# State-space tables of a two-block transformer kernel: read-out powers formed in the first feed forward, lags by shifted identities, drive tables in four buffers

## The reference, cut to what matters

```python
def modulation(cond, w_mod, b_mod):
    m = jax.nn.silu(cond) @ w_mod + b_mod          # 2048 x 6144 per layer
    ...
    h = rms_norm(x, norm_w[layer]) * (1.0 + scale) + shift
```

```python
    lam_bar = jnp.exp(lam * dt)                                   # 128 groups x 64 states, complex
    b_bar = ((lam_bar - 1.0) / lam)[..., None] * (b_re + 1j * b_im)
    c_mat = c_re + 1j * c_im
    ...
    y = jnp.einsum('bcgp,gip->bcgi', states, c_mat).real          # states by a scan along time
    y = y + d_skip * uf
```

## Time and profile before

| | us |
|---|---|
| median of 3 runs | 3765.3 |
| lowest and highest run | 3763.38, 3767.68 |
| the profiled execution's own time | 3764.49 |
| its span in the trace | 3762.70 |

### The profile page before, as it was taken

How to read it: one execution, slowest core, us unless ns; L and a number is a source line. 1 busy time by engine, 2 the same in 40 slices (tenths; PEclk the granted TensorE clock), 3 DMA queues, 4 the chain that set the end, 5 groups by cost and what they waited for, 6 DMA issues and landing times.

```text
span 3762.7 us, 50741 instructions
## 1 busy us (share of the span) xinstructions
PE 3669.4 (98%) x20771; PEld 2974.0 (79%) x20771; DVE 2477.3 (66%) x3663; ACT 1641.2 (44%) x2342; POOL 134.4 (4%) x214
## 2 busy tenths in 40 slices
PE   6999999999999999999999999999989999999999
PEld 3688887887888888556888888888878888888887
DVE  7877787578776666676766545655596566545654
ACT  4422333424445443434464434444545554434443
POOL 2000000100000010022000000000000000000000
PEclk9999999999999999999999999999989999999999
DMA  9766665255863576356656656655735556556664
GB/s 376 261 204 206 196 207 173 78 176 168 268 212 118 174 239 199 129 161 175 218 153 189 192 194 190 190 191 190 258 125 181 200 168 190 191 194 190 190 204 162
DMA packets 361063, 722.47 MB, mean 192 GB/s; under 512 B 32544, under 2 KB 34916, under 8 KB 355968
## 3 DMA queue, kind: packets, MB, share of 16 engines
q1 hardware_dynamic: 341344, 640.89, 53.6%
q0 software_dynamic: 17792, 76.07, 5.7%
q10 hardware_dynamic: 1696, 2.26, 0.2%
HBM read 689.34 MB, written 26.37 MB: 190 GB/s over the span
## 4 chain that ended last, share of the span: by engine, by line
PE 89%; DVE 6%; DMA 3%; ACT 2%; issue 1%; POOL 0%; SPq 0%; DVEq 0%; ACTq 0%; POOLq 0%
PE acc L1040 57%; PE acc L1610 7%; PE tp L1610 6%; PE acc L1608 4%; PE tp L1608 3%; PE tp L1085 2%; DMA ring<-in_w_mod 2%; PE tp L1275 1%; PE acc L1275 1%; PE acc L1680 1%; PE acc L1141 1%; DVE big L4247 1%; DVE prob_t L4247 1%; DVE ring_r L2929 1%; PE acc L1125 1%
## 5 line engine op out<-in xcount | busy, mean ns | idle before, releaser
L2929 DVE TENSOR_TENSOR ring_r<-ring,ring_r 128x1024 fp32r<-128x1024 f32 (+1 forms) x984 | 1188.5, 1217 | 951.9 <-ACT ring_r L1928 941.4
L1928 ACT ACTIVATE ring_r<-ring 128x1024 fp32r<-128x1024 f32 (+1 forms) x984 | 1030.0, 1054 | 1549.4 <-DMA ring<-in_ffn_down 387.4
L1040 PE MATMUL acc<-ring_r,feat_hi 128*128 128x512 f32 x2688 | 832.1, 391 | 4.7 <-DVE ring_r L2929 4.7
L1040 PE MATMUL acc<-ring_r,hid_t_hi 128*128 128x512 f32 x2048 | 630.8, 389 | 0.0
L1040 PEld LDWEIGHTS acc<-ring_r,feat_hi 128*128 128x128 f32 x2688 | 503.2, 188 | 115.4 <-DVE ring_r L2929 5.9
L1040 PE MATMUL acc<-ring_r,feat_lo 128*128 128x512 f32 x1344 | 524.0, 390 | 0.0
L1040 PEld LDWEIGHTS acc<-ring_r,hid_t_hi 128*128 128x128 f32 x2048 | 384.2, 188 | 79.5
L1040 PE MATMUL acc<-ring_r,hid_t_lo 128*128 128x512 f32 x1024 | 398.4, 389 | 0.0
L1610 PE MATMUL acc<-feat_pair,ring_r 128*128 128x512 f32 x1080 | 379.0, 394 | 0.0
L1610 PE MATMUL tp<-feat_pair,ring_r 128*128 128x512 f32 x960 | 336.7, 394 | 0.0
L1608 PE MATMUL acc<-feat_pair,ring_r 128*128 128x256 f32 x1152 | 309.5, 279 | 0.3
(11 more groups left out here) (565 smaller groups left out, 4155.3 us busy)
## 6 DMA issues: line engine op xcount, KB each, us to landing
ring<-in_ffn_up SPq DMA_DIRECT2D x256, 512.0 KB, 3.7
ring<-in_ffn_down SPq DMA_DIRECT2D x256, 512.0 KB, 3.6
ring<-in_w_mod SPq DMA_DIRECT2D x192, 512.0 KB, 4.9
ring<-in_w_in SPq DMA_DIRECT2D x176, 512.0 KB, 4.0
ring<-in_w_out SPq DMA_DIRECT2D x64, 512.0 KB, 3.7
ring<-in_even_w_in SPq DMA_DIRECT2D x64, 512.0 KB, 4.5
ring<-in_xattn_wkv SPq DMA_DIRECT2D x32, 512.0 KB, 4.5
ring<-in_even_w_out SPq DMA_DIRECT2D x32, 512.0 KB, 4.4
```

Source lines behind the costliest of these rows:

```text
L1040: mm = pe.matmul(bank[0:l.shape[-1], 0:width], l, r, start=(kk == 0 and j == 0), stop=(kk == g.kt - 1 and j == len(terms) - 1))
L1928: f(ring_r[:, slot, 0, 0:kt, 0:width], ring[:, slot, 1, 0:kt, 0:width], ACT.Copy) \
L2929: tt(lo, raw, hi, ALU.subtract).then_inc(sem("w_lo"), E.up("w_lo"))
```

## The change

- The drive tables get four buffers (`tb_B` by quarter). Their four spills, and the raw read-out table (`s_cr`, new, 1 MB), are issued by POOL behind the columns ("cols", 6). The spills of the lag tables stay among the modulations and follow `tt_ready`. A spill of the powers (`s_pwd`, new, 0.26 MB) and the small `s_ld2` go out at the first `r_ready`.
- `s5_read` is gone. Its 16 products (4 quarters by 4 powers) are made in `ffn(0)`: DVE takes one unit (`read_out_unit`) at the slab 5 of each of the 16 up chunks, from `c_pw` and `c_raw`, which POOL loads from `s_pwd` and `s_cr` behind the cross-attention; POOL spills each unit (0.26 MB) to `s_cd`.
- `s5_table_t` multiplies by the raw read-out table, 16 columns for 64. Its result goes through DVE once (the diagonal added, `tb_lag`), and PE then shifts it by four products with shifted identities (`tb_sh`, `s5_shift`), 4 products of 128x128 for each of two banks. ACT copies the two banks to `tb_T`.
- ACT's repeat (L2247) is gone.
- The pieces sit elsewhere: on PE, `s5_tables(q)` behind ("cols", q) takes the shift of quarter q-1, then table_b(q), then table_t(q); nothing is left within mods 4 and 5 or ahead of `in0`.
- The waits of the feature quads follow the new spills.

```diff
         tb_R = [view(2048 * i, 2, 16, S5_STEP, 16) for i in range(2)]
-        tb_B = [view(4096 + 2048 * i, 8, 2, P) for i in range(2)]
+        tb_B = [view(o, 8, 2, P) for o in (4096, 6144, 12288, 14336)]
...
+        C_UNITS = [(q, x) for q in range(4) for x in range(S5_STEP)]
...
+            pool.wait_ge(sem("r_ready"), 1)
+            dma(s_ld2, tb_l2.rearrange("p z c k -> p (z c k)"), "cond_in_cd0_out")
+            dma(s_pwd, tb_pw.rearrange("p x c k -> p (x c k)"), "cond_in_cd0_out")
             for j in range(4):
-                pool.wait_ge(sem("cc_ready"), L.due("cc_ready"))
-                if j == 0:
-                    dma(s_ld2, tb_l2.rearrange("p z c k -> p (z c k)"), "cond_in_cd0_out")
-                if j == 3:
-                    pool.wait_ge(sem("cols_full"), 8)
-                dma(s_cd[j], flat4(tb_C[j % 2][:, 1:]), "lam_in_cd1_out" if j % 2 else "cond_in_cd0_out")
-                pool.wait_ge(sem("bt_ready"), L.due("bt_ready"))
-                dma(s_bd[j], flat4(tb_B[j % 2]), f"bd_out{j % 2}")
-                if j:
-                    pool.wait_ge(sem("tt_ready"), L.due("tt_ready"))
-                    dma(s_td[j - 1], flat4(tb_T[(j - 1) % 2]), "bc_in_td0_out" if j % 2 else "td1_out_t_out")
-            pool.wait_ge(sem("tt_ready"), L.due("tt_ready"))
-            dma(s_td[3], flat4(tb_T[1]), "td1_out_t_out")
+                pool.wait_ge(sem("tt_ready"), L.due("tt_ready"))
+                dma(s_td[j], flat4(tb_T[j % 2]), "td1_out_t_out" if j % 2 else "bc_in_td0_out")
+            pool.wait_ge(sem("cols_full"), 7)
+            pool.wait_ge(sem("bt_ready"), L.due("bt_ready", 4))
+            for j in (0, 2, 1, 3):
+                dma(s_bd[j], flat4(tb_B[j]), f"bd_out{j % 2}")
+            dma(s_cr, tb_raw[1].rearrange("p z r i -> p (z r i)"), "lam_in_cd1_out")
...
+                    for j, x in C_UNITS:
+                        if x == 0:
+                            dma(c_raw.rearrange("p z r i -> p z (r i)"),
+                                s_cr.rearrange("p (z r) -> p z r", z=2)[:, :, 256 * j:256 * j + 256], "lam_in_cd1_out")
+                        pool.wait_ge(sem("cc_ready"), L.due("cc_ready"))
+                        dma(s_cd[j][:, 512 * x:512 * x + 512], c_out[:, 0].rearrange("p z r i -> p (z r i)"), "cond_in_cd0_out")
...
             def s5_table_t(q):
-                pe.wait_ge(sem("cc_ready"), E.due("cc_ready"))
-                pe.wait_ge(sem("rep_ready"), E.due("rep_ready"))
...
+            def s5_shift(q):
+                pe.wait_ge(sem("lag_ready"), E.due("lag_ready"))
+                for g in range(2):
+                    n, bank = tp_bank("act_tp")
+                    for b in range(S5_STEP):
+                        moved = ident[:, :] if b == S5_STEP - 1 else tb_sh[:, b]
+                        mm = pe.matmul(bank[:, b * P:(b + 1) * P], moved, tb_lag[:, g].rearrange("p n i -> p (n i)"), start=True, stop=True)
+                    to_act(n, mm)
+
+            def s5_tables(q):
+                if q:
+                    s5_shift(q - 1)
+                if q < 4:
+                    s5_table_b(q)
+                    s5_table_t(q)
...
-                if l == 0:
-                    s5_table_t(3)
...
+                         ("mod", 2): [lambda: x_scale(range(4)), lambda: s5_lags(0), lambda: s5_table_b(1)],
+                         ("mod", 3): [lambda: s5_lags(1), lambda: s5_table_b(2)],
+                         ("mod", 4): [lambda: s5_lags(2), lambda: s5_table_b(3)], ("mod", 5): [lambda: s5_lags(3)],
...
+            def read_out_unit(n):
+                q, x = C_UNITS[n]
...
+                for c in range(2):
+                    by = c_pw[:, x, c, 16 * q:16 * q + 16].unsqueeze(1).unsqueeze(3).to_broadcast([P, 2, 16, 16])
+                    tt(c_out[:, c], c_raw, by, ALU.mult).then_inc(sem("dve_step"), E.up())
...
+                tt(c_out[:, 0, 0], c_out[:, 0, 0], c_out[:, 1, 1], ALU.add).then_inc(sem("dve_step"), E.up())
+                tt(c_out[:, 0, 1], c_out[:, 0, 1], c_out[:, 1, 0], ALU.subtract).then_inc(sem("dve_step"), E.up())
                 mark("cc_ready")
...
+                        if l == 0 and s == 5:
+                            read_out_unit(half * g_up.n + c)
```

More of the change, by code:

```diff
@@ L282, in two_blocks @@
         s_ld2 = dram("s_ld2", (P, 4 * PAIRS))
+        s_pwd = dram("s_pwd", (P, S5_STEP * 2 * PAIRS))
+        s_cr = dram("s_cr", (P, 2 * PAIRS * 16))
         def shaped(v, *shape):
@@ L600, in two_blocks @@
         tb_drow = view(9344, P)
-        tb_T = [view(13312 + 1024 * i, 8, 2, S5_STEP, 16) for i in range(2)]
-        tb_pw = view(15360, S5_STEP + 1, 2, PAIRS)
+        tb_sh = view(9472, S5_STEP - 1, P)
+        tb_lag = view(9856, 2, 8, 16)
+        tb_T = [view(10240 + 1024 * i, 8, 2, S5_STEP, 16) for i in range(2)]
+        tb_pw = view(30176, S5_STEP, 2, PAIRS)
         tb_raw = [view(25088 + 2048 * i, 2, PAIRS, 16) for i in range(2)]
@@ L1230, in s5_table_t @@
                                 rows, r = slice(64 * g, 64 * g + 64), 2 * n + o
[L1231 to L1233 removed]
+                                mm = pe.matmul(banks[g][64 * o:64 * o + 64, n * 16:(n + 1) * 16], tb_R[q % 2][rows, z, r].rearrange("p a i -> p (a i)"),
+                                               tb_raw[1][rows, z, 16 * q + r, :], start=(z == 0), stop=(z == 1))
                                 if n == 7 and z == 1 and x == 1:
                                     mm.then_inc(sem("tp_full"), E.up("tp_full"))
[L1237 to L1239 removed]
+            def s5_shift(q):
[12 more added lines that the diff above has]
+                    s5_table_t(q)
+            s5_pieces = {("mod", 0): [s5_natural]}
+            s5_pieces |= {("cols", q): [lambda q=q: s5_tables(q)] for q in range(5)}
             def turn_quad(q):
@@ L2245, in s5_table_b, with s5_lags @@
                 act.nop().then_inc(sem("bt_ready"), E.count("bt_ready"))
-                lags = tb_R[q % 2].rearrange("p z r a i -> p (z r) a i")
-                f(lags[:, :, 0:S5_STEP - 1], lags[:, :, S5_STEP - 1:].to_broadcast([P, 32, S5_STEP - 1, 16]), ACT.Copy) \
-                    .then_inc(sem("rep_ready"), E.up("rep_ready"))
+            def s5_lags(q):
+                if q >= 2:
+                    act.wait_ge(sem("td1_out_t_out" if q % 2 else "bc_in_td0_out"), 16 * (1 if q % 2 else 5))
+                for g in range(2):
+                    bank = take_turn()[:, :].rearrange("p (b n i) -> p n b i", b=S5_STEP, i=16)
+                    f(tb_T[q % 2][:, :, g], bank, ACT.Copy).then_inc(sem("act_tp"), E.up("act_tp"))
+                act.wait_ge(E.last_sem(), E.last_count())
+                act.nop().then_inc(sem("tt_ready"), E.count("tt_ready"))
             def x_sums():
@@ L3225, in s5_masks @@
                             .then_inc(sem("dve_step"), E.up())
+                dve.memset(tb_sh[:, :, :], 0.0).then_inc(sem("dve_step"), E.up())
+                dve.wait_ge(E.last_sem(), E.last_count())
+                ts(tb_d16, tb_d16, tb_m[:, S5_STEP - 1:S5_STEP], None, ALU.mult).then_inc(sem("dve_step"), E.up())
+                halves = lambda v: v.rearrange("p (o m) -> p o m", o=2)
+                for b in range(S5_STEP - 1):
+                    n = 16 * (b + 1)
+                    dve.tensor_copy(halves(tb_sh[:, b])[:, :, 0:n], halves(ident[:, :])[:, :, 64 - n:64]).then_inc(sem("dve_step"), E.up())
             def times(src, by, j):
@@ L3243, in s5_drive @@
                 mark("r_ready")
-            def s5_read(q):
-                rs = slice(16 * q, 16 * q + 16)
-                if q >= 2:
-                    dve.wait_ge(sem("lam_in_cd1_out" if q % 2 else "cond_in_cd0_out"), 16 * (12 if q % 2 else 5))
-                dve.tensor_copy(tb_C[q % 2][:, 0], tb_raw[1][:, :, rs]).then_inc(sem("dve_step"), E.up())
-                for x in range(1, S5_STEP + 1):
-                    t = times(tb_raw[1][:, :, rs], tb_pw[:, x, :, rs], x)
-                    tt(tb_C[q % 2][:, x, 0], t[0][:, 0], t[1][:, 1], ALU.add).then_inc(sem("dve_step"), E.up())
-                    tt(tb_C[q % 2][:, x, 1], t[0][:, 1], t[1][:, 0], ALU.subtract).then_inc(sem("dve_step"), E.up())
-                mark("cc_ready")
@@ new lines, in s5_lags @@
+            def s5_lags(q):
+                for g in range(2):
+                    tt(tb_dd[:, g], tb_d16.unsqueeze(1).to_broadcast([P, 8, 16]), along(tb_d[:, g, 8 * q:8 * q + 8], 16), ALU.mult) \
+                        .then_inc(sem("dve_step"), E.up())
+                dve.wait_ge(E.last_sem(), E.last_count())
+                for g in range(2):
+                    tt(tb_lag[:, g], turned()[:, 0:P].rearrange("p (n i) -> p n i", i=16), tb_dd[:, g], ALU.add).then_inc(sem("tp_free"), E.up("tp_free"))
+                mark("lag_ready")
+                turn_skip(2)
```

106 lines of the change are left out of this document (50 added, 56 removed).

## The result

The changed kernel takes **3770.6 us** (median of 20 runs, 3767.05 to 3777.74), the kernel before 3764.6 in the same session (20 runs, 3761.82 to 3768.83). The ratio is 1.0014, with a 95% interval of 1.0008 to 1.0020: 6.0 us slower, where 5.8 us of gain were forecast. It lies outside the range (3750.5 to 3766.5), on the other side.

The account below looks back on a forecast made before the run. The start was taken as bound by DMA bytes. Bytes 12.5 less 5.7 us gave 6.8; plus 1.0 for the tail, less 2 for the clock, 5.8 us of gain: 3759 us, range 3750.5 to 3766.5.

Parts of the forecast that it names:

- Bytes: Modulation products 3 to 7: 4.98 MB fewer spills, 12.5 us gained if the DMA engines stay full.
- The hold: Behind modulation product 2: PE waits for ACT's banks behind x_scale, 63.3 to 68.6 us; DMA engines idle 3.9 us.
- Table_t(0), "can run from 51.9 to 54.0": Table product 0 on PE, ahead of modulation product 2: 2.1 us, by its record count of 128.
- The clock: PE behind the hold: table_t(1) and half of product 3 at half clock, 2 us lost.
- The price of 5 us: Clock loss behind the hold if every such stand is followed by a slow stretch; it would give 3762.
- Rounds of products 4 to 6: Modulation products 4 to 6: PE's round 12.5 us against 11.9 of DMA, 1.8 us lost over the three.
- The tail: From last modulation slab to in0: table_t(3) leaves, but the first low part limits the gain to 1.0 us.
- The late spills, 0: Four s_bd and s_cr behind the modulations: landed by 145 us, before the quads need them, no cost.
- The rival that they starve `in0`: Late spills hold DVE at quad 2 or 3; PE would stand 18 us, time 3777; chance 0.07.
- The read-out units, 0: Feed forward: 16 units, 34 us of DVE, costed 0; 34 us if the cover were gone.

Follow-up runs that it names:

- e5: The changed kernel with x_scale behind modulation product 5 and the four s_bd spills issued among the modulations as each table is ready: 3771.8 us.
- e1: The changed kernel with ACT's x_scale moved behind modulation product 5, from ahead of the banks of shift(0) and table_b(1): 3762.5 us.
- e6: The changed kernel with both x_scale behind modulation product 5 and table_t(0) within modulation product 2: 3758.8 us.
- e3: The changed kernel with table_t(0) moved within modulation product 2, behind its fourth slab: 3766.0 us.
- e8: e6 with 16 unread 128x128 products on PE just ahead of in0: 3756.7 us.
- e9: e8 with the low part of in0's first slab made on DVE ahead of the last modulation columns: 3756.65 us.
- e4: The changed kernel with each read-out unit's two products on DVE made four times over: 3770.9 us.
- e7: e6 with the raw read-out table s_cr spilled with the first tables rather than behind the last modulation slab: 3763.3 us.
- e10: e6 with the low part of in0's first slab made on DVE ahead of the last modulation columns, no unread products: 3757.1 us.
- e11: e1 with table_t(0) cut in two, rows 0 to 3 at the change's place, rows 4 to 7 within modulation product 2: 3757.8 us.

## Why the prediction was wrong

- **Bytes**: for bytes put into the stretch the size was right (e5 against e1: 9.3 us for 10.5 us of bytes). That taking them out would pay 12.5 us less the hold wasn't. Even in e6, without either stand, the last slab comes 7.4 us earlier than before.
- **The hold**: its place, its releaser and its length (5.3 us, forecast 5.3) were right. It came 5.0 us later. The DMA time that goes with it was not 3.9 us: from 70 to 90 us the engines lack 8.5, and they are empty from 78 to 82 us, while PE makes table_t(1) at the lower clock and frees no slot.
- **Table_t(0), "can run from 51.9 to 54.0", is the step that failed.** It started at 51.95 and ended at 58.0. I costed it by its record count and duration and had no term, and no rival, for a stand in which PE waits for nothing that the profile names (3.54 us). In the kernel before, the eight slabs of product 2 come between table_b(0) and this table, and no such stand shows. In the change the slabs in flight have all landed before the stand is over, and the ring dries out: 250 GB/s in that window. By e3 the step is worth 4.6 us of the 11.6 between forecast (3759) and result (3770.6), with the 1.38 us of waiting for ACT ahead of it. That e6's time is the forecast's is chance: the forecast had the hold in it, e6 hasn't.
- **The clock**: 2 us forecast behind the hold, 2.5 found there (table_t(1) took 3.6 us for 2.1, product 3 6.3 for 5.3). So this term was about right; left out was the same price at the other two stands, 1.2 us in product 2 (6.5 for 5.3; the clock fell already in the table ahead of it, 0.84 from 53 to 54 us) and 1.5 in `in0`'s first slab (7.0 for 5.6). The rule that I weighed (the Trainium skill, "TensorE: Matmul & The Clock Gate", "Part 1: The HAM clock gate (the "warmup" mystery)") is that the throttled state is the default and that activity releases it; the trace agrees in that a slow stretch follows each of the three stands, of 3.5, 5.3 and 2.0 us. The price of 5 us that the prediction set beside it was for the hold alone, and there it was too high; that the three stretches add up to 5.2 is chance. With it the forecast would have been 3762, still 8.6 too low.
- **Rounds of products 4 to 6**: 12.5 us forecast, 13.3, 12.3 and 14.2 found; the last slab was taken 9.0 us after the end of product 6 rather than 7.5. Together 3.8 us. In these the slabs arrive one by one again, and product 6 has a slow stretch of its own behind a stand of 1.45 us. The DMA term was too small: from 100 to 120 us the engines show shares of 1.02 and 1.01 and move 363 and 357 GB/s, before 407 and 398 at 1.04. A round's 4.72 MB at 360 GB/s are 13.1 us (an estimate) rather than 11.9. Why a byte took longer isn't shown.
- **The tail**: 1.0 us forecast, 1.5 found (5.3 us from last slab to `in0`, before 6.7). But what left it, table_t(3), had kept PE busy while DVE made the first low part. In its place are 2.04 us of standing and the slow first slab (1.5 us in the change, 2.3 in e6, 0 in e8). I had reckoned the start of `in0`, not its clock. The trace of before had a sign of it: table_t(3) took 3.50 us for 2.1, at granted clocks of 0.66 and 0.50 from 132 to 136 us. The slow stretch behind the columns was there already, and fell on a piece with DVE's work beside it:

```profile
132.91 3.50 PE L1232 MATMUL tp<-big 64*64 64x64 f32 x128
```

- **The late spills, 0**: right in e8, where `in0` takes the old time with all five beside it. In the profiled run of the change PE stands 0.45 and 0.88 us at the quads, in e1 0.2 and in e9 1.0, in the others not; whether the spills are the cause isn't shown. The five land in 12.7 us (s_bd, median) and 19.1 us (s_cr), before 160 us rather than 150. The rival that they starve `in0` is out.
- **The read-out units, 0**: right (e4), and the waits of PE from 1880 to 2620 us are the old ones (1.0, 1.0 and 0.5 us) with one of 0.2 added.

The account against the forecast's `in0` at 130.5 us: 5.0 for table_t(0) and the slow product behind it, 0.5 for the clock behind the hold, 3.8 for the rounds and the last slabs, less 0.5 for the tail, is 8.8 (139.3). With 3.2 within `in0` it is 12.0 us; the medians are 3770.6 - 3759 = 11.6 apart.

## What to carry to other kernels

A stage that is bound by transfers through a ring gets faster with fewer bytes only while the consumer frees slots again before the slabs in flight have landed. Eight slabs are 10.6 us by their bytes, but here the cover was shorter: in the change PE frees no slot between 47.8 and 58 us, and the engines run dry from 56 on; in e6 6.9 us without a freed slot (60.8 to 67.7) already leave them at a share of 0.48 from 68 to 70 us. So when bytes are taken out, look for the longest stretches in which the consumer frees nothing, work and stands together, and break these first. A piece that is moved off the path may have been the cover of a hand-over and of the clock behind it: reckon what PE does in its place. And a stand costs its length plus the slow stretch that follows, in this kernel 1 to 4 us each time that PE was the bound.

## What was not expected of the hardware

PE can stand while it waits for no engine and no transfer that the profile names. In all five profiled runs with the whole of table_t(0) at the change's place, it stood 3.0 to 4.1 us at the same two last records; in e3, e6, e7, e8, e9 and e10, with it within product 2, it stood so for 0.4 us at most (e10, in table_t(2)). The guess is its supply of instructions. The DMA view has two queues called instruction, q8 and q14. In the change, the windows of 0.25 us from 55.00 and from 56.50 show their packets within the stand (54.2 to 57.7 us):

```profile
q8 instruction: 1, 0.02, 28.0%
...
q14 instruction: 1, 0.01, 11.3%
```

In e1 they fall at 56.0 and 56.5 us, within its stand of 54.6 to 58.7, in e11 at 56.0 and 56.75; in e6 the first is at 52.75, 4 us before PE passes the point. It is the same in others: in the six profiled kernels that stand the q8 packet comes between 55.0 and 56.5 us, in e3 and in the kernel before, which don't, between 51.0 and 52.0. That PE stood for a late piece of code fits these rows; that it did isn't shown, nor which engine's code each packet carries, nor why it is asked for earlier in e6. That the packet waited behind slabs is at most a part: when q8's packet comes the slabs fill the engines (share 1.06 from 54 to 55 us), but in the last 1.7 us of the stand they are nearly empty (0.36 and 0.10 from 56 to 58), and PE stands on. The Trainium skill, "Runtime: NRT & Kernel Launch", section "Instruction fetch mechanics", says that the sequencer fetches its program in blocks of 16 KiB by its own DMA queue while it runs the present one, and that the cost of crossing a block is mostly hidden. The 0.02 MB of q8's packet agree with the size, the 0.01 of q14's don't. In the kernel before, e3 and e6 such packets come without a stand, as the page has it; if the stand in the other six is such a crossing, there the cost was not hidden.
